# Encoder block: the fourth x tile is turned by VectorE and a DRAM trip too, and the order of SP's queue around it changes

## The reference: what is computed

```python
h = rmsnorm(x, norm_mix[l])
proj = jnp.einsum('bsd,dc->bsc', h, w_in[l])
qa, ka, va, ga, cq, ckv, kr, gb = jnp.split(proj, split_idx, axis=-1)
...
q = jnp.einsum('bsc,ce->bse', rmsnorm(cq, q_a_norm[l]), w_uq[l])
...
kv = jnp.einsum('bsc,ce->bse', rmsnorm(ckv, kv_a_norm[l]), w_ukv[l])
```

## Time and profile before

| | us |
|---|---|
| median of the runs | 604.01 (603.74 to 604.06) |
| the profiled execution | 603.7 |
| its span | 601.9 |
| PE busy | 593.2 (99%) |
| PE's weight loads busy | 483.3 (80%) |
| DVE busy | 448.5 (75%) |
| ACT busy | 355.9 (59%) |
| POOL busy | 292.9 (49%) |

### The profile page before, as it was taken

How to read it: one execution, slowest core, us unless ns; L and a number is a source line. 1 busy time by engine, 2 the same in 40 slices (tenths; PEclk the granted TensorE clock), 3 DMA queues, 4 the chain that set the end, 5 groups by cost and what they waited for, 6 DMA issues and landing times.

```text
span 601.9 us, 9190 instructions
## 1 busy us (share of the span) xinstructions
PE 593.2 (99%) x3068; PEld 483.3 (80%) x3068; DVE 448.5 (75%) x806; ACT 355.9 (59%) x762; POOL 292.9 (49%) x273
## 2 busy tenths in 40 slices
PE   8999999999999999999999999999999999999996
PEld 7888888888888888888887777777777777888885
DVE  5777563334434439998999788998998988799884
ACT  6645132213333238777886678788788788434563
POOL 4610702515756432535547536777787776510601
PEclk9999999999999999999999999999999999999999
DMA  7698458684776620101015966767777745698043
GB/s 245 192 283 231 135 135 282 213 295 127 262 261 228 209 70 2 36 1 36 2 27 115 256 151 181 196 175 194 192 176 192 201 129 184 209 366 317 1 164 117
DMA packets 74911, 102.11 MB, mean 170 GB/s; under 512 B 13416, under 2 KB 45680, under 8 KB 74864
## 3 DMA queue, kind: packets, MB, share of 16 engines
q1 hardware_dynamic: 74704, 101.25, 56.7%
q10 hardware_dynamic: 160, 0.27, 0.1%
HBM read 60.17 MB, written 31.62 MB: 153 GB/s over the span
## 4 chain that ended last, share of the span: by engine, by line
PE 93%; DVE 2%; ACT 2%; DMA 1%; POOL 1%; issue 1%; SPq 0%; ACTq 0%
PE ps L1911 18%; PE ps L1913 18%; PE ps L1912 18%; PE ps L2204 9%; PE ps L2182 8%; PE ps L2112 5%; PE ps L2117 5%; PE ps L2082 3%; PE ps L2132 2%; PE ps L2092 2%; PE ps L2069 2%; PE ps L2068 2%; PE ps L2093 2%; DMA wn_raw<-w_in 1%; POOL wn_lo L779 1%
## 5 line engine op out<-in xcount | busy, mean ns | idle before, releaser
L1761 DVE TENSOR_TENSOR pT_lo<-ps,pT_hi 128x512 fp32r<-128x512 f32 x102 | 69.3, 684 | 21.3 <-ACT pT_hi L1286 20.2
L1911 PE MATMUL ps<-hT_hi,w_hi 128*128 128x512 f32 x208 | 84.0, 404 | 0.0
L1913 PE MATMUL ps<-hT_hi,w_lo 128*128 128x512 f32 x208 | 81.4, 391 | 0.0
L1912 PE MATMUL ps<-hT_lo,w_hi 128*128 128x512 f32 x208 | 81.1, 390 | 0.0
L1273 ACT ACTIVATE p_b<-ps,stat 128x1024 f32<-128x1024 f32 x64 | 71.3, 1114 | 12.5 <-DVE stat L1736 12.1
L1736 DVE TENSOR_REDUCE stat<-ps 128x1 f32<-128x1024 f32 x64 | 76.5, 1212 | 2.2 <-PE ps L2132 2.0
L1286 ACT ACTIVATE pT_hi<-ps 128x512 fp32r<-128x512 f32 x102 | 60.4, 596 | 23.7 <-PE ps L2182 23.4
L2182 PEld LDWEIGHTS ps<-ident,p_b 128*128 128x128 f32 x408 | 48.8, 140 | 17.4 <-issue 5.2
L2182 PE MATMUL ps<-ident,p_b 128*128 128x128 f32 x408 | 61.9, 275 | 0.6 <-DVE pT_lo L1761 0.4
L823 POOL TENSOR_SCALAR p_w<-p_w,stat 128x384 f32<-128x384 f32 (+1 forms) x40 | 24.4, 623 | 55.3 <-DVE stat L1644 55.3
L939 POOL TENSOR_TENSOR pT_lo<-p_land,pT_hi 128x512 fp32r<-128x512 f32 x26 | 33.4, 1290 | 31.4 <-ACT pT_hi L1293 31.4
(11 more groups left out here) (241 smaller groups left out, 1505.6 us busy)
## 6 DMA issues: line engine op xcount, KB each, us to landing
w_raw<-w_in SPq DMA_DIRECT2D x13, 512.0 KB, 4.0
probs_scratch<-p_blk SPq DMA_DIRECT2D x52, 128.0 KB, 2.8
p_land<-probs_scratch SPq DMA_DIRECT2D x13, 512.0 KB, 4.5
x_in<-x SPq DMA_DIRECT2D x8, 512.0 KB, 3.9
wt_raw<-w_out SPq DMA_DIRECT2D x8, 512.0 KB, 4.5
t_scratch<-wt_hi SPq DMA_DIRECT2D x16, 256.0 KB, 2.7
t_scratch<-wt_lo SPq DMA_DIRECT2D x16, 256.0 KB, 3.0
q<-q_h SPq DMA_DIRECT2D x16, 256.0 KB, 3.7
```

The source lines that it names most:

```text
L1761: nc.vector.tensor_tensor(pT_lo[at_], ps[:, 4 + a, :].rearrange("p (k c) -> p k c", c=P), f(pT_hi[at_]), ALU.subtract).then_inc(s_bTl, 1)
L1911: nc.tensor.matmul(o, a_hi, b_hi, start=first, stop=False, skip_group_check=goes_on)
L1912: nc.tensor.matmul(o, a_hi, b_lo, start=False, stop=False, skip_group_check=goes_on)
L1913: return nc.tensor.matmul(o, a_lo, b_hi, start=False, stop=last, skip_group_check=goes_on)
```

## The change

`X_PE` becomes 3, so tile 3 takes the second way. TensorE's `turn_x(3)` goes. Tile 3's landing place is row 4 of `latT_hi`; its fetch counts on the semaphore of `g_row`. The block buffer of even tiles moves from 147 to 201 KB, so `lat_norm(0)` and `lat_norm(1)` no longer wait for x stores. All latents use one block buffer, `lat_b`, so `lat_norm(1)` waits for the stores of the latents before it. On VectorE h_lo(3) stands behind norm_x(6), lat_norm(0) and h_lo(4) between norm_x(7) and turn_blocks(7). On ScalarE h_hi(3) stands behind square_x(6). On SP store_x(3) stands ahead of load_x(6), the gains and fetch_x(3) behind it, fetch_x(4) ahead of store_x(5), and store_x(7) behind store_lat(0). lat_stats(4) waits for the last x store of the odd tiles.

```diff
--- before.py
+++ after.py
@@ -62,7 +62,7 @@
 BASE = 16512
-X_PE = 4
+X_PE = 3
 ACT_UNITS = range(2, 16, 2)
...
@@ -113,7 +113,7 @@
         sq_l = at("sq_l", 154, [P, QL])
-        lat_b, lat_b1 = (at(name, kb, [P, 4, LT, Q32]) for name, kb in (("lat_b", 142.5), ("lat_b1", 161)))
+        lat_b = at("lat_b", 142.5, [P, 4, LT, Q32])
         kr_n = at("kr_n", 152, [P, NT, ROPE])
...
@@ -124,7 +124,7 @@
 
-        x_blk = [at(f"x_blk{i}", kb, [P, 4, KT, Q32]) for i, kb in enumerate((147, 161))]
+        x_blk = [at(f"x_blk{i}", kb, [P, 4, KT, Q32]) for i, kb in enumerate((201, 161))]
 
...
@@ -236,7 +236,7 @@
         s_wnh, s_wnr = sem("wn_hi_ready"), sem("wn_ready")
-        s_grow, s_gcol, s_gT, s_gb = sem("g_row_in"), sem("g_col_ready"), sem("g_turned"), sem("g_broadcast")
+        s_grow, s_gcol, s_gT, s_gb = sem("g_row_then_fourth_tile_in"), sem("g_col_ready"), sem("g_turned"), sem("g_broadcast")
         s_pA, s_pB = sem("natA_done"), sem("natB_done")
...
@@ -390,7 +390,9 @@
 
-            a, r = ((latT_hi, 0), (latT_hi, 2), (latT_lo, 0), (latT_lo, 2))[t - X_PE]
+            if t == X_PE:
+                return f(latT_hi[:, 4, :]).rearrange("p (r c) -> p r c", r=2)
+            a, r = ((latT_hi, 0), (latT_hi, 2), (latT_lo, 0), (latT_lo, 2))[t - X_PE - 1]
             return f(a[:, r:r + 2, HALF:SEQ])
...
@@ -436,8 +438,7 @@
             load_wn(7)
-            sp.dma_start(g_q[:, :], q_a_norm.partition_broadcast(P)).then_inc(s_glat, 16)
-            sp.dma_start(g_kv[:, :], kv_a_norm.partition_broadcast(P)).then_inc(s_glat, 16)
+
             def store_x(t):
...
@@ -448,29 +449,32 @@
                 sp.dma_start(x_turned(t), xt_scr[t - X_PE].rearrange("a p (r q) c -> (a p) r (q c)", r=2)) \
-                    .then_inc(s_xq[t - X_PE], 16)
-
+                    .then_inc(s_xq[t - X_PE - 1] if t > X_PE else s_grow, 16)
+
+            store_x(3)
             load_x(6)
+            sp.dma_start(g_q[:, :], q_a_norm.partition_broadcast(P)).then_inc(s_glat, 16)
+            sp.dma_start(g_kv[:, :], kv_a_norm.partition_broadcast(P)).then_inc(s_glat, 16)
+            fetch_x(3)
             store_x(4)
             load_x(7)
+            fetch_x(4)
             store_x(5)
-            fetch_x(4)
             store_x(6)
             fetch_x(5)
-            store_x(7)
 
...
                 sp.wait_ge(s_lblk, t + 1)
-                b = lat_b1 if t == 1 else lat_b
                 for q in range(4):
                     sp.dma_start(lt_scr[t, :, :, q, :].rearrange("a p c -> p a c"),
-                                 b[q * Q32:(q + 1) * Q32].rearrange("p a k c -> p a (k c)")).then_inc(s_lout, 16)
+                                 lat_b[q * Q32:(q + 1) * Q32].rearrange("p a k c -> p a (k c)")).then_inc(s_lout, 16)
 
...
             store_lat(0)
+            store_x(7)
             fetch_x(6)
...
@@ -1011,7 +1015,7 @@
                 if t >= X_PE:
-                    act.wait_ge(s_xq[t - X_PE], 16)
+                    act.wait_ge(s_xq[t - X_PE - 1], 16) if t > X_PE else act.wait_ge(s_grow, 32)
                     for r in range(2):
...
@@ -1091,7 +1095,7 @@
                 if t == 4:
-                    act.wait_ge(s_lout, 128)
+                    act.wait_ge(s_xsto[1], 192)
                 nc.scalar.activation(vA[:, t, :, 0:HD], ps[:, a, 0:P].rearrange("p (g c) -> p g c", c=HD),
...
@@ -1127,11 +1131,11 @@
             square_x(4)
-            h_hi(3)
             wn_hi_k(6)
...
             square_x(6)
+            h_hi(3)
             square_x(7)
...
@@ -1468,8 +1472,6 @@
                     dve.wait_ge(s_latT, t - 1)
-                else:
-                    dve.wait_ge(s_xsto[t], 128)
                 dve.wait_ge(s_lrms, t + 1)
...
@@ -1479,9 +1481,9 @@
                 dve.wait_ge(s_lat, t + 1)
-                if t >= 2:
-                    dve.wait_ge(s_lout, 64 * (t - 1 if t == 2 else t))
-                nc.vector.transpose((lat_b1 if t == 1 else lat_b)[:, :, :, :],
+                if t >= 1:
+                    dve.wait_ge(s_lout, 64 * t)
+                nc.vector.transpose(lat_b[:, :, :, :],
                                     lat[:, t % 2, :].rearrange("p (k a c) -> p a k c", a=4, c=Q32)).then_inc(s_lblk, 1)
...
@@ -1524,10 +1526,9 @@
             h_lo(0, range(1, 2))
-            for t in range(1, 4):
+            for t in range(1, X_PE):
                 norm_x(t)
-                if t < 3:
-                    h_lo(t)
+                h_lo(t)
             def turn_blocks(t):
...
@@ -1537,11 +1538,12 @@
                 norm_x(t)
+                if t == 6:
+                    h_lo(3)
+                if t == 7:
+                    lat_norm(0)
+                    h_lo(4)
                 turn_blocks(t)
-                if t == 4:
-                    h_lo(3)
-            lat_norm(0)
-            h_lo(4)
 
...
@@ -1977,7 +1979,6 @@
             both(2, range(4))
-            turn_x(3)
             for k in (4, 5):
...
```

## The result

The changed kernel takes 607.92 us (median of 6 runs, 606.78 to 611.65) against 604.15 for the kernel before on the same chip (6 runs, 603.74 to 604.73): ratio 1.0068, 95% interval 1.0054 to 1.0082. The forecast was 604.6, with 606.5 as the upper end. The profiled execution takes 607.87 us, its span is 606.1 where it was 601.9: +4.2.

What follows compares the result with a forecast made beforehand. TensorE, busy 593.2 of 601.9 us, was taken as the bound. Removing transposes gives -0.88, but a queue delay of 1.2 less 0.6 slack gives +0.6 on 604.01: 604.6 us, range 603.1 to 606.5.

Steps and rivals of the forecast that it cites:

- the gain: TensorE, fourth x tile: removing eight transposes saves 0.88 us, giving 603.1 if kept in full; chance of full gain 0.21.
- d: Delay down SP's queue to the load of uq_raw and on to the last q latents; taken as 1.2 us.
- store_lat(1) +1.1, fetch_lat(1) +1.2 to +1.4: SP's queue: second latents, turned 1.0 us later, delay their store and fetch by these us, then the uq_raw load.
- Rival 2: DMA rings are the bound: uq_raw slides by most of 3.7 us, total +1.9 to +3.1, 606.5 in the middle; chance 0.20.
- uq_raw after 56.5: SP's queue: sign for the full rings; the forecast itself expected the uq_raw load at 55.5 to 56 us.
- The one buffer: Single latent buffer: no cost beyond the 1.0 us later second latents, as store_lat(0) has landed by 49 us.
- max(-0.88, d - 0.6): After the seventh up-projection: change of the total is the larger of the transposes' gain and d less 0.6 us slack.
- Rival 3: TensorE before natural(3): tile 3 late from slow store or fetch, 1 to 2 us lost, total 604.1 to 605.1; chance 0.13.
- weight row 7: GpSimd's part comes about 0.9 us later; costs TensorE 0 to 0.5, taken 0.3, not added since later waits swallow it.
- Slower by over 0.2%: Whole kernel: outcome more than 0.2% (1.2 us) slower; chance 0.28.
- chain without slack: Latents' links from uq_raw to the last q latents: no slack until 0.6 us before the seventh up-projection.
- rings at 0.95 of their time: 16 DMA engines busy 0.95 from 26 to 38 us, where both added transfers fall; cited for the full-rings rival.

Runs made afterwards that it cites:

- e2_store5_first: Changed kernel with store_x(5) put back ahead of fetch_x(4) in SP's queue; 605.95 us, ratio 1.0021 to the kernel before.
- e8_before_extra: Kernel before with two unused 512 KB loads ahead of load_x(6), awaited by SP ahead of fetch_lat(0); 605.2 us, ratio 1.0017.
- e3_two_buffers: Changed kernel with a second block buffer for the second latents, so lat_norm(1) doesn't wait; 608.59 us, ratio 1.0071 to the kernel before.
- e13_after_again: The changed kernel run once more, unaltered; 608.1 us, ratio 1.0055 to the kernel before.
- e14_front: e9_full with weight row 7 rounded between square and root of tile 5, and g_q, g_kv issued behind fetch_x(3); 604.5 us, ratio 1.0006.
- e4_both: Changed kernel with store_x(5) ahead of fetch_x(4) and a second latent buffer; 606.97 us, ratio 1.0039 to the kernel before.
- e12_dummy: Changed kernel with eight unused identity transposes on TensorE where turn_x(3) stood; 605.56 us, ratio 1.0032 to the kernel before.
- e5_uq_later: Changed kernel with the load of uq_raw moved behind store_lat(2); 606.83 us, ratio 1.0046 to the kernel before.
- e1_keep_busy: Changed kernel with 20 identity transposes on TensorE ahead of the seventh up-projection; 607.14 us, ratio 1.0046 to the kernel before.
- e6_all: Changed kernel with store_x(5) ahead of fetch_x(4), a second latent buffer and uq_raw behind store_lat(2); 605.22 us, ratio 1.0022.
- e9_full: e6_all with the first rope_k moved behind last_norm and ScalarE's wait for it gone; 603.91 us, ratio 1.0000 to the kernel before.
- e10_before_rope: Kernel before with only the first rope_k moved behind last_norm; 604.19 us, ratio 1.0002.

## Why the prediction was wrong

It held that the gain would be spent at the seventh up-projection and that SP's queue would carry a delay d into uq_raw and from there to the last q latents. Place and path were right. The size was not.

- **Up to the first latents the reckoning held.** Turned at 45.4 against 45.0 forecast; norm_x(4) slow beside GpSimd (2.45); tile 7 in at 39.5 against 39.
- **The step that failed: "From there the delay runs down SP's queue: store_lat(1) +1.1, fetch_lat(1) +1.2 to +1.4", and with it d = 1.2.** It let VectorE's later second latents set the pace. Measured were +2.91, +4.74 and a d of 4.74 (4.85 relative to the load of tile 5). Two terms stood at nothing. One is SP's own time: it stood for 4.0 us at fetch_x(4), then issued eight stores in 5.12 us, and from 45.83 it issued without a pause up to store_lat(1). The other is a slower landing of that store, 3.90 us for 2.25.
- **What of it is shown.** The prediction named the queue ("store_x(4), load_x(7), fetch_x(4) stand behind fetch_x(3)") and didn't ask what waits behind fetch_x(4): store_x(5), whose tile was ready. e2_store5_first puts that right, uq_raw goes out 1.8 us earlier, and the time falls beyond the intervals. What store_x(7) costs between the stores of the first and the second latents (2.17 us of issuing) is tested by no run: every version of the change keeps it there.
- **The rings.** Rival 2's 3.7 us was taken as the upper end of d, and its own test, uq_raw after 56.5, was met at 59.2. A megabyte of loads alone makes 2.5 (e8_before_extra), but along another way than in the changed kernel, so 2.5 and 1.8 can't be added up. A d above either alone speaks for queue and rings together, where the prediction had set them as alternatives; how they share it stays open.
- **The one buffer costs nothing, but not for the reason given.** store_lat(0) had not landed by 49; VectorE waited 1.58 us. It is harmless because SP couldn't have sent the second latents sooner (e3_two_buffers).
- **d doesn't pass one for one.** By "max(-0.88, d - 0.6)" a d of 4.74 would give +4.1. The chain arrived 2.82 late and TensorE 2.36: the later links do have slack, against what was said, above all in SP's four issues for the last q latents (1.90 for 3.25). That the total came out at +4.2 all the same is two errors that cancel.
- **What was never considered: the clock.** Behind the gap it fell to 0.50 and took 1.68 us in the profiled execution. Without it the change costs some 2.1 us (the four runs of e13_after_again with the full clock, median 606.2, against 604.06 of before on that chip), about the wait of 2.36 and the size of rival 2.
- **Rival 3 and weight row 7.** Tile 3's low part was 0.30 late, row 7 0.28, within the bounds given. But "isn't added up, since later waits swallow it" hid that two small waits take 0.58 of a gain of 0.88 even if all else goes well. e14_front shows they can be removed.
- **Smaller slips.** Four issues of a store were taken as 1.4 us (26.0 to 27.4) and took 2.41 (25.91). By the prediction's own terms tile 3 has 1.4 to spare at a fetch of 4.1, not 1.2, and is 2.3 late with the slowest store, not 2.0; and 1.4 against 1.25 gives d = -0.15 as its lower bound, not -0.4. None of these moves the forecast.
- **Chances.** Slower by over 0.2% had 0.28 and came true. The "chain without slack" and rings at 0.95 of their time were both in the text; a chance of 0.46 for a d of 1.2 rested on the queue alone.

The Trainium skill (TensorE: Matmul & The Clock Gate, section "What's actually happening") says that the clock's default state is the throttled one and that activity releases it, judged on a pattern of time that runs on freely of the program. The trace agrees in the levels (0.50 and 1.00). The two groups of e13_after_again fit the second part, with 6 of 10 executions of one kernel at the lower mean clock, but no run here shows it.

## What to carry to other kernels

When an engine at 99% is relieved of work by a trip through DRAM, the price stands in the queue that issues the trip and in the rings: go through the new order of that queue one entry at a time, ask of each wait when what it waits for was issued, count SP's own issuing (1.9 to 2.4 us for a store in four pieces here), and don't take the traffic and the queue as alternatives. Don't put a fetch directly behind the stores it waits for while other stores are ready. Once the busy engine has to wait about 2 us at one place, count the lower clock behind the gap as well, and look for two groups in the times.

## What the runs showed of the hardware that was not expected

- Behind idle gaps of 1.93 to 3.38 us (e4_both, e2_store5_first, e3_two_buffers, e12_dummy, e13_after_again, e5_uq_later) the mean clock was 0.996 or less in some executions of each kernel and 0.997 or more in others, and the profiled ones at the lower mean show the granted clock at 0.50 behind the gap (the changed kernel, e4_both); with gaps of 0.46 to 1.76 us (e1_keep_busy, e6_all, e9_full) none of 27 executions had a mean clock below 0.997. It isn't proof of a threshold: each gap is known from one execution, and one of 31 executions of the kernel before and one of 10 of e10_before_rope, neither with such a gap in its trace, had 0.995.
- Four tensor_tensor operations of 128x80 on VectorE took 0.65 us together alone (the changed kernel) and 2.11 to 2.20 beside GpSimd's splitting of uq_raw (e5_uq_later, e6_all).
- In the trace of the change a four-piece store costs SP 1.9 to 2.4 us of issuing, and eight pieces in a row 5.12: 0.64 us a piece. A single issue of x took 0.33 to 0.43 us, and 0.87 behind such a store.
